# First attention of a two-block transformer kernel: value halves as two 64-column weights with three summed products, instead of one 128-column weight with two products and an addition

## The reference, cut to what matters

```python
o_cmp, p_cmp = compressed_attention(q, kcc, vcc)      # 31 compressed keys
sel_idx = select_blocks(p_cmp, S)                     # top 8 of 8 blocks: all of them here
o_sel = selected_block_attention(q, ks, vs, sel_idx)  # causal over 512 keys
o_win = banded_attention(q, kw, vw, NSA_WINDOW, None) # window 512: causal over 512 keys
o = g[..., 0:1] * o_cmp + g[..., 1:2] * o_sel + g[..., 2:3] * o_win
return o.reshape(B, S, qd) @ w_out
```

## Time and profile before

| What | us |
|---|---|
| Time before, median of 3 runs | 2686.83 |
| Lowest and highest of them | 2684.83, 2690.34 |
| Span of the profiled execution | 2688.4 |
| TensorE busy in it | 2526.6 (94%) |
| VectorE busy | 1344.7 (50%) |
| ScalarE busy | 716.3 (27%) |
| GpSimd busy | 1761.7 (66%) |

### The profile page before, as it was taken

One profiled execution on the slowest core, in us unless ns is written; L12 is line 12 of the kernel. 1 busy time (PEld: TensorE's weight loads), 2 busy tenths in 40 slices (PEclk: granted clock), 3 DMA queues, 4 the chain that ended last, 5 costly groups with the idle time before them and its releaser, 6 DMA issues. The chain is left out here.

```text
span 2688.4 us, 36565 instructions
## 1 busy us (share of the span) xinstructions
PE 2526.6 (94%) x11854; PEld 2049.3 (76%) x11854; DVE 1344.7 (50%) x2632; ACT 716.3 (27%) x1504; POOL 1761.7 (66%) x977
## 2 busy tenths in 40 slices
PE   8898889899999978899998999999999889999998
PEld 6787677688888767688886877777877777787877
DVE  6467887443342575411213566664138434751552
ACT  4205776201101254301112222222016232100001
POOL 4464445587777576577776545455769777687884
PEclk9998889999999989999999999999999999999999
DMA  7681001264653202233332321212423213233332
GB/s 268 190 234 59 1 1 32 94 195 150 195 187 95 62 24 90 70 94 102 94 95 78 97 60 55 62 57 64 109 83 70 82 52 121 81 101 91 90 103 75
DMA packets 420546, 259.73 MB, mean 97 GB/s; under 512 B 62845, under 2 KB 411514, under 8 KB 414018
## 3 DMA queue, kind: packets, MB, share of 16 engines
q1 hardware_dynamic: 395024, 199.47, 25.6%
q10 hardware_dynamic: 25393, 58.63, 6.6%
HBM read 253.86 MB, written 8.10 MB: 97 GB/s over the span
## 5 line engine op out<-in xcount | busy, mean ns | idle before, releaser
L669 POOL TENSOR_TENSOR W<-RAW,zeros 128x1024 fp32r<-128x1024 f32 (+2 forms) x349 | 667.4, 1912 | 656.1 <-PE PA L753 311.1
L676 POOL TENSOR_TENSOR W<-RAW,W 128x1024 fp32r<-128x1024 f32 (+2 forms) x355 | 850.5, 2396 | 50.2 <-PE PA L761 12.7
L750 PE MATMUL PA<-H,W 128*128 128x512 f32 x1288 | 505.0, 392 | 6.4 <-POOL W L669 1.9
L753 PE MATMUL PA<-H,W 128*128 128x512 f32 x1288 | 502.4, 390 | 0.0
L750 PE MATMUL PA<-A,W 128*128 128x512 f32 x944 | 373.5, 396 | 16.5 <-DVE A L2008 10.8
L753 PE MATMUL PA<-A,W 128*128 128x512 f32 x944 | 371.6, 394 | 0.0
L761 PE MATMUL PA<-H,W 128*128 128x512 f32 x1288 | 318.3, 389 | 0.0
L750 PEld LDWEIGHTS PA<-H,W 128*128 128x128 f32 x1288 | 241.9, 188 | 60.9 <-POOL W L669 6.3
L753 PEld LDWEIGHTS PA<-H,W 128*128 128x128 f32 x1288 | 241.8, 188 | 50.2 <-issue 0.5
L761 PEld LDWEIGHTS PA<-H,W 128*128 128x128 f32 x1288 | 241.7, 188 | 50.1
L761 PE MATMUL PA<-A,W 128*128 128x512 f32 x944 | 238.5, 395 | 0.0
(11 more groups left out here) (374 smaller groups left out, 3947.6 us busy)
## 6 DMA issues: line engine op xcount, KB each, us to landing
AD<-in_ada_w_dram ACTq DMA_DIRECT2D x40, 1024.0 KB, 5.1
RAW<-in_w_in_dram SPq DMA_DIRECT2D x160, 256.0 KB, 3.2
RAW<-in_mlp_w_up_dram SPq DMA_DIRECT2D x128, 256.0 KB, 3.1
RAW<-in_mlp_w_down_dram SPq DMA_DIRECT2D x128, 256.0 KB, 3.1
RAW<-in_w_up_dram SPq DMA_DIRECT2D x88, 256.0 KB, 3.1
RAW<-in_nsa_w_in_dram SPq DMA_DIRECT2D x40, 256.0 KB, 4.2
RAW<-in_w_down_dram SPq DMA_DIRECT2D x16, 384.0 KB, 3.4
RAW<-in_swa_w_in_dram SPq DMA_DIRECT2D x20, 256.0 KB, 3.4
```

Source lines behind the costliest of these rows:

```text
L669: e.tensor_tensor(W[0][:, s, 0:kc], RAW[:, s, 0:kc], zeros[:, 0:1].rearrange("p (a b) -> p a b", b=1).broadcast_to([P, kc, P]), ALU.add).t ...
L676: e.tensor_tensor(W[1][:, s, 0:kc], RAW[:, s, 0:kc], W[0][:, s, 0:kc].bitcast(F32), ALU.subtract).then_inc(w_split, 1)
L750: pe.matmul(PA[s][:, 0:n], W[0][:, s, k], hi, start=(k == 0), stop=False)
L753: mm = pe.matmul(PA[s][:, 0:n], W[0][:, s, k], lo, start=False, stop=False)
```

## The change

The 128-column weight is given as two weights of 64 columns, its high half (y = 0) and its low half (y = 1). For each key block there are three products in place of two: high weights with the high and with the low values, low weights with the high values. The product of the two low parts, which the kernel before has in its sum, is left out. All three go to rows 0 to 63 of `PO`. The output is of the kind "kept": VectorE copies 64 rows, and ScalarE's copy is gone.

```diff
-                    values=[(VV[1 if n else g % 2 * 2][:, t, :], x, t, t, NT) for t in range(NT) for x in range(2)],
+                    values=[(VV[1 if n else g % 2 * 2][:, t, y * HD:y * HD + HD], x, t, t, NT) for t in range(NT) for x, y in ((0, 0), (0, 1), (1, 0))],
...
-                need=[("q", h)], need_v=("v", 2, 0), head=h, first=False, out=("halves", OF[(h % 2) * HD:(h % 2) * HD + HD, h // 2, :]), rows=NCMP,
+                need=[("q", h)], need_v=("v", 2, 0), head=h, first=False, out=("kept", OF[(h % 2) * HD:(h % 2) * HD + HD, h // 2, :], 0), rows=NCMP,
...
-                values=[(VC2[:, g, :], x, 0, 0, NT) for x in range(2)],
+                values=[(VC2[:, g, y * HD:y * HD + HD], x, 0, 0, NT) for x, y in ((0, 0), (0, 1), (1, 0))],
...
-                        mm = pe.matmul(PO[hd % 2][:, a * P:z * P], v, turned[x][0:grp["rows"], rows + slot, a * P:z * P],
+                        mm = pe.matmul(PO[hd % 2][0:v.shape[-1], a * P:z * P], v, turned[x][0:grp["rows"], rows + slot, a * P:z * P],
```

## The result

The changed kernel took 2695.48 us (median of 13 runs, 2689.39 to 2703.15), the kernel before 2685.13 us beside it (13 runs): +10.4, ratio 1.0034 with a 95% interval of 1.0027 to 1.0041. It is slower, as forecast, and within the range; the forecast was 2701.

What follows compares the result with a forecast made beforehand. VectorE bounds the stage before; with the change TensorE would. Ordinary heads +10, waits +1, heads after group changes +3 and the stage's end +0.8 sum to +14.8, less about 1: +14, 2701 us, range 2691 to 2709.

Steps and rivals of the forecast that it cites:

- Switches of the shape of the weights: TensorE pauses going to and from 64-column weights: six more visits a head at 0.33 us, 2.0 us.
- the +10 for ten ordinary heads: TensorE needs 13.0 us an ordinary head, above the present 12.0, so ten take 130 us in place of 119.9.
- Wrong: Listed counter-signs: value products following transposes at once, ordinary heads near 12 us with TensorE waiting, or loss at group changes.
- columns alone: Rival: no pauses at new switches, scores a few tenths late a head; +2 to +6, about 2691; chance 0.12.
- Columns: Value products on TensorE stream 3072 more columns a head, 1.4 us; 64-column weights shorten nothing.
- The heads after a change: Three heads following a key/value head change lose about 1 us more each to TensorE's lower clock: +3, between 0 and +6.
- The clock rival: Pauses absent, fuller TensorE keeps its upper clock, ordinary heads 11.0 to 11.5 us: -4, 2683; chance 0.05.
- Output: VectorE's copy replaces its addition at like cost: 0; ScalarE loses 595 ns a head: 0.
- The end of the stage: Last 16 products become 24, +1.2; last compressed product +0.2; ScalarE's copy gone, -0.6: together +0.8.

Runs made afterwards that it cites:

- wide3: The change with three products per key block kept, but all 128 columns as weights; 2696.49 us, ratio 1.0034 to the kernel before.
- narrow2: The change with only two 64-column products per key block, the low half of the values left out; 2686.79 us, ratio 0.9995 to the kernel before.
- fill3: The change plus eight zero-weight 512-column products on TensorE at each of three key/value head changes; 2684.28 us, ratio 0.9974 to the kernel before.
- before_fill: The kernel before plus 3 x 8 zero-weight products on TensorE at the changes of key/value head; 2686.37 us, ratio 1.0003 to the kernel before.

## Why the prediction came out as it did

- **Sign and range** were right: 2695.5 in 2691 to 2709, slower by 0.34%. The sum behind them was not: its largest term measured nothing.
- **The step that failed is "Switches of the shape of the weights", 6 x 0.33 = 2.0 us a head.** It measured nothing. wide3 and the change have the same stage, and 27 products need 10.9 us of TensorE, 9.5 + 1.4, not 13.0. With it the +10 for ten ordinary heads falls: their need stays below the 11.3 us that VectorE sets, and at full clock nearly all of the columns is covered (0.1 us longer, the last head 0.4). The rows that it rested on, were plain 32-bit products with 62 columns, and the pause there does not carry over. The rule of the Trainium skill that stood beside them ("TensorEngine Tiling", Key Properties), read as the prediction read it, would also have drained TensorE at 128x64; at the new products the trace does not agree, and the measurement decides. Two of the signs that the prediction listed under "Wrong" came: value products that follow the transposes at once, and ordinary heads near 12 us with TensorE waiting. The rival "columns alone", given 0.12, has the stage's length, +2 to +6 (measured +4.2), but not its place: it expected a few tenths in every head, and three heads took the loss, through the clock.
- **Columns**, 1.4 us a head: right (1.37). That 64-column weights shorten nothing holds for the long products; where a part ends with one of 128 columns, the scores follow after 0.06 us in place of 0.11.
- **The heads after a change**, +3 for the clock: cause and size were right (+3.5), and fill3 shows the cause, since filled they differ by 0.1 each. The working was not: it took a need of 13.0 us and a missing share of 0.17. The length can be worked out from what was measured: a granted clock of 0.76 over 14.27 us means 6.8 us at the lower level, which costs half of that, 3.4; 10.9 + 3.4 = 14.3. Before, a loss of this sort (0.75 in one of the three heads) met a need of 9.5 under the 11.2 us of a filled head and was partly covered.
- **The clock rival** (0.05) was half right: the fuller TensorE does keep its clock in ordinary heads (11.29 at 1.00 against 12.01 at 0.86), which gave back what other heads lost. It is why the seven come out even, and why the rival's price alone was no forecast.
- **Output**: VectorE's copy takes 0.68 us, as the addition did: 0, right. ScalarE's 595 ns, 0: right within the 1.0 to 2.7 us by which narrow2's stage is shorter; its time is that of before. But the step did not ask what the other choice would bring: copied by ScalarE, the same rows save 11.8 us of the stage (217.1 to 205.3). With the waits filled in both, 6.6 of it stay (207.5 to 200.9), which is about what VectorE's relief is worth by itself; the rest went with the clock.
- **The end of the stage**: +0.8 forecast; from the last compressed score products (436.3 before, 442.4 after) to the start of the last copy it is 9.9 us before and 10.6 after, +0.7.
- **What no term held** is the +4.2 behind the stage; the prediction let the stage's loss alone reach the end. That the total came into the range was luck in good part: 4.2 us in the stage for 14.8 forecast, and as much again in code that no term looked at.

## To carry to other kernels

A pause seen at one kind of product is no price for another: before a term of 10 us rests on such rows, look whether type, rows and waits are the same. Ask for every engine how long it needs for a unit of work, and compare with the longest of them: 1.4 us more on the second engine cost 0.1 in most heads while it had 1.7 to spare, and moving 0.68 us off the first one was worth more than the whole change. Where TensorE waits for another engine ahead of work that it bounds, work without use in that wait can pay for itself, because the clock that it keeps is worth half of the lower stretch; whether the gain reaches the end has to be read from the time, as fill3 (0.9974) and before_fill (1.0003) show.

## What was not expected of the hardware

The eight 64-column products of the earlier stage took 0.46 us from the first start to the last end where they lay in two column halves, and 0.68 when all lay in one:

```profile
109.88 0.68 PE L1145 MATMUL PS<-hid,PHI 128*64 128x62 f32 x8
```

So products in different halves ran beside each other there. And 31-row weights pause TensorE on both sides (0.09 and 0.12 us above), while 64-column fp32r weights with 128 rows do not (0.03 us in, and no more than the streamed columns out).
